# DeltaNet rounds: the zeros of the power products and the unit matrices are written by ScalarE in place of GpSimd

## The reference, cut to what matters

```
lower = where(strict, (k_beta @ k.T) * decay, 0)
T = triangular_solve(eye + lower, eye, lower=True, unit_diagonal=True)
u, w = T @ v_beta, T @ (k_beta * exp(g))
step: v_new = u - w @ S;  o = q_decay @ S + intra @ v_new;  S = S * g_last + k_tail.T @ v_new
```

## Time and profile before

| | us |
|---|---|
| median of 3 runs | 2858.31 |
| lowest, highest | 2855.41, 2859.74 |
| profiled execution, own time | 2854.43 |
| its span | 2852.7 |
| mean granted clock of TensorE | 0.939 of full speed |

### The profile page before, as it was taken

How to read it: one execution, slowest core, us unless ns; L and a number is a source line. 1 busy time by engine, 2 the same in 40 slices (tenths; PEclk the granted TensorE clock), 3 DMA queues, 4 the chain that set the end, 5 groups by cost and what they waited for, 6 DMA issues and landing times.

```text
span 2852.7 us, 42525 instructions
## 1 busy us (share of the span) xinstructions
PE 2591.7 (91%) x16620; PEld 2345.8 (82%) x16620; DVE 2101.5 (74%) x2663; ACT 1211.4 (42%) x1596; POOL 242.9 (9%) x290
## 2 busy tenths in 40 slices
PE   1189999778888999999999989998989999999998
PEld 1188887777786889888988989998968898889887
DVE  7778999788758777777777888557877755555556
ACT  0135555433346443344344453454364434443444
POOL 0002222222200000000000101000000000000000
PEclk6589999877889999999999999999999999999998
DMA  9854443445545888887888669654858755555552
GB/s 337 296 208 145 148 144 118 153 155 163 174 153 176 281 282 277 271 278 276 284 280 282 231 222 361 216 164 150 283 187 278 249 192 192 190 184 196 190 186 88
DMA packets 291420, 616.03 MB, mean 216 GB/s; under 512 B 23211, under 2 KB 23746, under 8 KB 291010
## 3 DMA queue, kind: packets, MB, share of 16 engines
q1 hardware_dynamic: 258626, 488.04, 51.0%
q0 software_dynamic: 32640, 125.84, 12.7%
HBM read 611.73 MB, written 2.10 MB: 215 GB/s over the span
## 4 chain that ended last, share of the span: by engine, by line
PE 80%; DVE 12%; issue 4%; ACT 2%; DMA 1%; SPq 1%; DVEq 0%; POOL 0%; ACTq 0%
PE groups L2391 12%; PE groups L2395 12%; PE groups L2393 12%; PE groups L2383 11%; PE groups L2385 11%; PE groups L2387 11%; PE pc L2561 2%; DVE ada_acc L813 1%; DVE ada_acc L1899 1%; DVE w_lo L1917 1%; PE pm L2358 1%; PE pb L2550 1%; SPq L1553 1%; PE pa L1054 1%; DMA w_raw<-in_ab_w_in_dram 1%
## 5 line engine op out<-in xcount | busy, mean ns | idle before, releaser
L1632 ACT ACTIVATE w_hi<-w_raw 128x1024 fp32r<-128x1024 f32 x776 | 817.1, 1059 | 1216.8 <-PE groups L2387 546.0
L1917 DVE TENSOR_TENSOR w_lo<-w_raw,w_hi 128x1024 fp32r<-128x1024 f32 x749 | 909.5, 1223 | 559.2 <-ACT w_hi L1632 555.3
L2383 PE MATMUL groups<-w_hi,act_hi 128*128 128x512 f32 x1408 | 554.5, 394 | 23.8 <-DVE act_lo L2047 23.8
L2391 PE MATMUL groups<-act_hi,w_hi 128*128 128x256 f32 x1776 | 518.6, 292 | 39.5 <-DVE act_lo L2047 13.1
L2387 PE MATMUL groups<-w_lo,act_hi 128*128 128x512 f32 x1408 | 550.8, 391 | 0.0
L2385 PE MATMUL groups<-w_hi,act_lo 128*128 128x512 f32 x1408 | 550.7, 391 | 0.0
L2393 PE MATMUL groups<-act_lo,w_hi 128*128 128x256 f32 x1776 | 510.6, 288 | 0.0
L2395 PE MATMUL groups<-act_hi,w_lo 128*128 128x256 f32 x1776 | 509.9, 287 | 0.0
L2391 PEld LDWEIGHTS groups<-act_hi,w_hi 128*128 128x128 f32 x1776 | 349.0, 197 | 52.3 <-issue 44.1
L2391 PE MATMUL groups<-hid_hi,w_hi 128*128 128x256 f32 x1392 | 388.5, 279 | 0.0
L2395 PE MATMUL groups<-hid_hi,w_lo 128*128 128x256 f32 x1392 | 386.8, 278 | 0.0
(11 more groups left out here) (408 smaller groups left out, 2653.4 us busy)
## 6 DMA issues: line engine op xcount, KB each, us to landing
ada_units<-in_ada_w_dram POOLq DMA_DIRECT2D x120, 1024.0 KB, 6.4
w_raw<-in_ffn_w_gate_dram SPq DMA_DIRECT2D x88, 1024.0 KB, 5.2
w_raw<-in_ffn_w_up_dram SPq DMA_DIRECT2D x88, 1024.0 KB, 5.3
w_raw<-in_ffn_w_down_dram SPq DMA_DIRECT2D x88, 1024.0 KB, 5.2
w_raw<-in_cd_w_in_dram SPq DMA_DIRECT2D x48, 1024.0 KB, 5.3
w_raw<-in_ab_w_in_dram SPq DMA_DIRECT2D x40, 1024.0 KB, 5.2
ada_units<-in_ada_w_dram SPq DMA_DIRECT2D x80, 512.0 KB, 4.8
ada_first<-in_ada_w_dram SPq DMA_DIRECT2D x24, 1024.0 KB, 10.2
```

What stands on the lines that cost most here:

```text
L1632: act.activation(whi[:, half, k], raw[:, slot, k], ACT.Copy).then_inc(hi_done, 1)
L1917: dve.tensor_tensor(wlo[:, half, k], raw[:, slot, k], whi[:, half, k].bitcast(F32), ALU.subtract).then_inc(lo_done, 1)
L2383: pe.matmul(dst, hi[:, k, rows], whi[:, j % 2, kk], start=(k == 0), stop=False, skip_group_check=True)
L2391: pe.matmul(dst, whi[:, j % 2, kk, cols], hi[:, k], start=(q == 0 and kk == 0 and n % 2 == 0), stop=False, skip_group_check=True)
```

## The change

ScalarE gets the two kinds of work, with a mark each: `zero{i}.{k}` right after the power copy of each level, as an activation with a scale of 0.0 on a tile of ones, and `init{i}` (two activations that copy the unit matrix to d and to dt). `init0` stands in the prelude after the fourth side split and ahead of `glu_tanh(0)`; `init{i+1}` stands at the end of round i, ahead of `exp_norm(i+1)`. GpSimd loses the copies and the memsets. In place of its wait for the copies it waits, ahead of mb of level 0, for the last power product of the round before. TensorE's wait for the clearing moves from ahead of y to between y and x.

```diff
 def act_names():
-    names = [..., "stq0", "stk0", "tv0", "tz0"]
+    names = [..., "stq0", "stk0", "init0", "tv0", "tz0"]
...
-        names += [f"p{i}.0"] + ([f"vn0{i - 1}"] if i else [])
+        names += [f"p{i}.0", f"zero{i}.0"] + ([f"vn0{i - 1}"] if i else [])
...
-        names += [f"p{i}.6"] + ([f"stq{i + 1}", f"stk{i + 1}"] if nxt else []) + (...)
+        names += [f"p{i}.6", f"zero{i}.6"] + ([f"init{i + 1}"] if nxt else []) + ([f"stq{i + 1}", f"stk{i + 1}"] if nxt else []) + (...)
...
+            def power_zero(i, k):
+                odd = blocks4(power(i, k), k)[:, :, :, 1]
+                even_ones = ones[:].unsqueeze(1).broadcast_to([P, 4, P])
+                done(act.activation(odd, blocks4(even_ones, k)[:, :, :, 0], ACT.Copy, scale=0.0), f"zero{i}.{k}")
+
+            def unit(i):
+                unit4 = ident[:].unsqueeze(1).broadcast_to([P, 4, P])
+                if i:
+                    on(dne, f"p{i - 1}.{LEVELS - 1}")
+                act.activation(d[:], unit4, ACT.Copy)
+                done(act.activation(dt[:, i % 2], unit4, ACT.Copy), f"init{i}")
...
             side_split(3)
+            unit(0)
             glu_tanh(0)
...
                     power_copy(i, k)
+                    power_zero(i, k)
                     if k == 0 and i:
...
                 if nxt:
+                    unit(i + 1)
                     exp_norm(i + 1)
...
 level (VectorE), power_up (TensorE):
                     if k == 0:
-                        on(dnp, f"init{i}")
+                        on(dna, f"init{i}")
...
             def add_up(i, k):
                 on(dna, f"p{i}.{k}")
-                on(dnp, f"zero{i}.{k}")
...
                 if k < LEVELS - 1:
                     each_half(pc, [...], f"y{i}.{k}")
+                on(dna, f"zero{i}.{k}")
                 each_half(pb, [...], f"x{i}.{k}")
...
             for i in range(ROUNDS):
-                if i:
-                    on(dne, f"p{i - 1}.{LEVELS - 1}")
-                if i > 1:
-                    on(dne, f"vn1{i - 2}")
-                pool.tensor_copy(d[:], all4(ident[:]))
-                done(pool.tensor_copy(dt[:, i % 2], all4(ident[:])), f"init{i}")
                 on(dnd, f"m{i}")
                 for k in range(LEVELS):
-                    if k:
-                        on(dne, f"p{i}.{k - 1}")
+                    if k or i:
+                        on(dne, f"p{i}.{k - 1}" if k else f"p{i - 1}.{LEVELS - 1}")
                     done(pool.tensor_tensor(mb[:], m[:], all4(lm[:, k]), ALU.mult), f"mb{i}.{k}")
-                    done(pool.memset(blocks4(power(i, k), k)[:, :, :, 1], 0.0), f"zero{i}.{k}")
```

More of the change, by code:

```diff
@@ L119, in act_names @@
 def act_names():
-    names = ["tq0", "tk0", "sqq0", "sqk0", "gx0", "dm0", "bx0", "ed0", "lnq0", "lnk0", "stq0", "stk0", "tv0", "tz0"]
+    names = ["tq0", "tk0", "sqq0", "sqk0", "gx0", "dm0", "bx0", "ed0", "lnq0", "lnk0", "stq0", "stk0", "init0", "tv0", "tz0"]
     for i in range(ROUNDS):
@@ L124, in act_names @@
         names += [f"gx{i + 1}"] if nxt else []
-        names += [f"p{i}.0"] + ([f"vn0{i - 1}"] if i else [])
-        names += [f"p{i}.1"] + ([f"hi{i - 2}"] if i > 1 else []) + ([f"dm{i + 1}", f"bx{i + 1}", f"ed{i + 1}"] if nxt else []) + ([f"S{i - 1}"] if i else [])
-        names += [f"p{i}.2"]
-        names += ([f"ks{i - 1}"] if i else []) + [f"p{i}.3"] + ([f"tq{i + 1}", f"tk{i + 1}"] if nxt else [])
+        names += [f"p{i}.0", f"zero{i}.0"] + ([f"vn0{i - 1}"] if i else [])
+        names += [f"p{i}.1", f"zero{i}.1"] + ([f"hi{i - 2}"] if i > 1 else []) + ([f"dm{i + 1}", f"bx{i + 1}", f"ed{i + 1}"] if nxt else []) + ([f"S{i - 1}"] if i else [])
+        names += [f"p{i}.2", f"zero{i}.2"]
+        names += ([f"ks{i - 1}"] if i else []) + [f"p{i}.3", f"zero{i}.3"] + ([f"tq{i + 1}", f"tk{i + 1}"] if nxt else [])
         names += [f"vn1{i - 1}"] if i else []
-        names += [f"p{i}.4"] + ([f"oc{i - 1}"] if i else [])
+        names += [f"p{i}.4", f"zero{i}.4"] + ([f"oc{i - 1}"] if i else [])
         names += [f"sqq{i + 1}", f"sqk{i + 1}", f"tv{i + 1}", f"tz{i + 1}"] if nxt else []
-        names += [f"p{i}.5"] + ([f"lnq{i + 1}"] if nxt else []) + ([f"ss{i - 1}"] if i else [])
+        names += [f"p{i}.5", f"zero{i}.5"] + ([f"lnq{i + 1}"] if nxt else []) + ([f"ss{i - 1}"] if i else [])
         names += ([f"lnk{i + 1}"] if nxt else []) + ([f"lnr{i - 1}"] if i else [])
-        names += [f"p{i}.6"] + ([f"stq{i + 1}", f"stk{i + 1}"] if nxt else []) + ([f"exr{i - 1}", f"on{i - 1}"] if i else [])
+        names += [f"p{i}.6", f"zero{i}.6"] + ([f"init{i + 1}"] if nxt else []) + ([f"stq{i + 1}", f"stk{i + 1}"] if nxt else []) + ([f"exr{i - 1}", f"on{i - 1}"] if i else [])
         names += [f"rr{i}", f"kt{i}"]
@@ L163, in pool_names @@
     for i in range(ROUNDS):
-        names += [f"init{i}"]
         for k in range(LEVELS):
-            names += [f"mb{i}.{k}", f"zero{i}.{k}"]
+            names += [f"mb{i}.{k}"]
             if k == 2 and i + 1 < ROUNDS:
```

## The result

The change made the kernel slower by 0.19%: ratio 1.0019, 95% interval 1.0012 to 1.0025, median 2863.88 us against 2858.49 over 16 runs each. That is 5.4 us, where -0.1 was forecast. The profiled execution of the changed kernel spans 2863.9 us, 11.1 more than that of before. Half of this is not the change: its prelude already begins 3.5 us later, and 1.8 us are added after the last round. (A second trace of the kernel before begins its prelude 3.1 us later than the first.) What can be compared is the stretch between: from the table load for the two exps in the prelude (526.68 in the trace of before, 530.16 after) to the out turn of round 3 (790.89 and 800.23). It takes 264.2 us before and 270.1 after, **+5.9**, about what the medians show.

A forecast was written before the change was run, and what follows sets the result against it. VectorE was taken as the fullest engine in the rounds, outside the weight stream. ScalarE's +2.22 us against VectorE's -2.34 gave -0.1, so 2858.2 us from the median of 2858.31; range 2852.5 to 2864.5.

The forecast's parts named there:

- the clock case: Rival: longer TensorE idle at boundary 1/2 sends two more levels into the lower clock, +7 us, 2865; chance 0.08.
- Prelude: Before round 0: the first unit pair delays the gate's tanh, and VectorE's L848 waits for it, +0.60 us.
- L629's delay: Round boundaries: clearing and unit pair delay the scaled rows by 1.33 us, in full at 1/2, nothing at 0/1 and 2/3.
- the clearing on the path at the end: After round 3's last power copy: the out turn waits for ScalarE, which has only the clearing added, +0.29 us.
- a tensor_scalar: Rounds: VectorE tensor_scalars held by GpSimd's memset go 0.26 us earlier without it; six count, -1.56 us.
- boundary 0/1: Between rounds 0 and 1: VectorE no longer stretched by GpSimd's unit-matrix copies, -0.23 us; ScalarE's delay absorbed by 3.7 of slack.
- The limited rule: Port pair: two-input VectorE instructions contend only with GpSimd ones that read SBUF; tensor_scalar also with writes: 0.26 us back, others none.
- The unlimited form: Rival: all memsets hold VectorE whatever the form; the other 16 stretched operations give 0.26 each, -4.2 us, 2854.0; chance 0.07.
- The slack of 0.05 at boundary 2/3: Between rounds 2 and 3: 1.93 us of slack, less VectorE's gain of 0.55 and ScalarE's delay of 1.33; nothing lost.
- The rival that ScalarE binds every boundary: Rival: VectorE's freed time makes L629 last at all three boundaries, +3.8 us, 2862; chance 0.09.
- Mid-level clearing at nothing: Inside each level: clearing on ScalarE costs nothing, covered between y and x; without cover up to 0.29 us per level.
- the idle time before that gram: Sign at boundary 1/2: TensorE's idle before round 2's gram product grows from 2.06 us to near 3.4.

The follow-up runs named there:

- the three fills: Change as made plus sixteen unread TensorE products ahead of the gram product alone, at each boundary, against the kernel before: ratio 0.9971, stretch 254.8 us.
- with all: Change as made plus unread products, eight ahead of each power product from level 1, sixteen ahead of gram, against the kernel before: ratio 0.9944, 2842.46 us.
- the doubled pair: Whole change, only the first unit pair early, plus an unneeded second pair in the prelude, against the kernel before: ratio 0.9996, stretch 267.4, again 263.6 us.

## Why the prediction was wrong, point by point

- **The range held, the forecast did not.** 2863.88 lies inside 2852.5 to 2864.5, but the forecast was no change, with 0.84 on it, and the measured 0.19% is clear of zero, at the edge of what I had called measurable. That the range held is luck: it left the clock case out, and by the ledger it was the clock that used it up.
- **ScalarE's and GpSimd's terms held.** Prelude +0.61 for +0.60, L629's delay 1.33 for 1.33, the clearing on the path at the end +0.30 for +0.29 (last power copy to L635: 5.07 us before, 5.37 after), a tensor_scalar 0.25 for 0.26 (five of the six counted), boundary 0/1 -0.22 for -0.23, two-input forms unchanged. The limited rule of the Trainium skill, page "SBUF — State Buffer", section "Who interferes with whom", agrees with the trace (1.38 and 1.39 us with and without the memset; 1.76 and 1.51 for tensor_scalar). The unlimited form is out.
- **The slack of 0.05 at boundary 2/3** was as thin as it was said to be: gram now waits for ScalarE there. VectorE's gain came (six accumulations take 4.83 us for 5.40), but gram starts only 0.23 us earlier after the level's power product, not 0.55: the power copy came 0.21 later, behind a power product at the lower clock, and ScalarE ended last. A further 0.32 went into a slower gram (2.05 for 1.73), so this boundary came out at +0.09 for -0.55. The rival that ScalarE binds every boundary thus came true at two of three; its +3.8 charged the prelude 1.04 where the sum has 0.60.
- **Mid-level clearing at nothing** held: no wait of TensorE for it between y and x was seen, and the version with the clearing alone is not slower.
- **The step that failed** is the one that made a sum at all: "That delays L629 by 0.29 + 1.04 = 1.33 ... +1.33 in full, as TensorE's gram, turns, sums, side and level 0 follow without a gap", with "a microsecond won or lost at their end should go through". It took TensorE's durations as fixed, and the sum had nothing for the clock. They follow the granted clock, and the clock follows TensorE's own idle time (0.77 in the rounds of the changed kernel, 0.83 with the three fills, 0.97 with all). At boundary 1/2 the added wait came out as 1.3 us of its own and 0.7 of slower products right behind it, +2.05 in all, and the other pieces took more than their terms: rounds 0 and 1 by 1.8 us, round 2 and its boundary by 1.3, round 3 and the end by 2.1. By run times the pairs between rounds cost 6.0 us where 1.33 was the term.
- **The signs.** GpSimd's memsets and copies are gone from the rounds, the clearing takes 0.41 us with the next start 0.31 behind it, and ScalarE releases the gram of round 2 and the out turn. Two signs failed: the idle time before that gram is 4.97 us, not near 3.4, and the rounds, counted as in the earlier trace rows, take 248.5 us, not 243 within 3.
- **The rival that came true** is the clock's, priced at +7 (2865) and given 0.08. Its mechanism was right in kind, its condition only in part: it asked for more levels at the lower clock, and the clock's mean did not fall (0.76 and 0.77). The levels that are low are others, and some of them are less well covered by VectorE (level 4 of round 3 above; level 3 of round 2 is covered in full). That its +7 lies near the measured +5.4 is luck. It deserved far more than 0.08, since the earlier trace rows showed the clock at three quarters and single products at 219 to 447 ns.

## What to carry to other kernels

Where a stage runs at a mean granted clock between its two levels, TensorE's durations are not constants: after a change of one microsecond in the order of work other levels can be the slow ones, and the outcome can be several times the sum of the terms. The same program can also take more than one course, so compare run times and not two single traces. Look at the granted clock of the stage first; if it is near three quarters because TensorE waits, giving it unneeded products in those waits (here 0.6% of the kernel, in 250 us of it) is worth more than moving small operations between engines, up to the point where they outlast the wait. And put moved work where the receiving engine idles: the same instructions a few places later cost nothing.

## What was not expected of the hardware

- The same program often gets the same pattern of low clock: two traces of the change as made agree to 0.02 us in 258, and two of the kernel before to 0.5 us. But a program can have more than one course (267.4 and 263.6 us for the doubled pair), and the same instructions in round 0 took 54.68 us in one version and 55.91 in another.
- Level 2 of round 3 takes 6.17 us at a granted clock of 0.72 and 8.67 at 0.50, level 4 takes 6.73 at 1.00 and 9.30 at 0.63, with VectorE busy for 4.3 to 4.7 and for about 6.4 us. Level 3 of round 2, with VectorE busy for 9.25, takes 9.50 at 1.00 and at 0.64.
- In single traces delays did not add (-0.2 and +2.3 us apart, +6.3 together), while the run times of the same versions did, within their intervals (0.9 and 6.0, together 6.6 to 7.1).
- Added work made the kernel faster: 480 matrix instructions more, 18 us less (2840.24 against 2858.7 beside it).
